# Page gathers issued once x has landed, compression weights loaded behind the first ada block, ada steps of the projection two tiles later

## What is computed

```
mod  = silu(c) @ w_ada + b_ada              # 2048 x 12288; shift1, scale1, gate1, shift2, scale2, gate2
h    = rmsnorm(x, norm1_g) * (1 + scale1) + shift1
p    = h @ w_in                             # queries, keys, values, gates, merge gates
past = cache_cmp_kv[page_table]             # 8 sequences x 16 pages x 128 rows: 2 MB each sequence
kvc  = gelu(blocks(past) @ cmp_w1 + pe @ cmp_w1) @ cmp_w2      # compression of the cached keys and values
m    = mixer(p, kvc, caches)                # compressed, selected, window and dilated attention
x    = x + gate1 * (m @ w_out)
x    = x + gate2 * swiglu(rmsnorm(x, norm2_g) * (1 + scale2) + shift2)
y    = rmsnorm(x, normf_g)
```

## Time and profile before

| | us |
|---|---|
| median of 3 runs | 1949.8 (1948.12 to 1950.07) |
| the profiled execution, its own time | 1946.32 |
| its span, first to last instruction | 1944.5 |
| PE busy | 1853.2 (95%) |
| DVE / ACT busy | 976.4 / 750.3 |
| mean granted PE clock | 0.980 |

### The profile page before, as it was taken

One profiled execution on the slowest core, in us unless ns is written; L12 is line 12 of the kernel. 1 busy time (PEld: TensorE's weight loads), 2 busy tenths in 40 slices (PEclk: granted clock), 3 DMA queues, 4 the chain that ended last, 5 costly groups with the idle time before them and its releaser, 6 DMA issues.

```text
span 1944.5 us, 35691 instructions
## 1 busy us (share of the span) xinstructions
PE 1853.2 (95%) x15365; PEld 1698.7 (87%) x15365; DVE 976.4 (50%) x1622; ACT 750.3 (39%) x1101; POOL 58.3 (3%) x108
## 2 busy tenths in 40 slices
PE   6988999999998879999999989999999999999997
PEld 4556899999954556999999989999999999999996
DVE  3437456654357533644456674444444444745454
ACT  2437333344344432533334343333333333633332
POOL 0000000000000000000000000000000000000000
PEclk9999999999999889999999999999999999999998
DMA  9991888887699857987788857777788777788881
GB/s 387 405 378 45 288 250 259 242 234 185 193 422 420 338 206 274 279 260 233 252 248 293 272 203 272 269 259 266 274 272 284 263 259 235 244 295 275 274 277 45
DMA packets 336549, 516.66 MB, mean 266 GB/s; under 512 B 8914, under 2 KB 310394, under 8 KB 319658
## 3 DMA queue, kind: packets, MB, share of 16 engines
q1 hardware_dynamic: 316306, 370.56, 57.4%
q0 software_dynamic: 5248, 125.73, 16.5%
q10 hardware_dynamic: 14896, 18.96, 3.6%
HBM read 506.32 MB, written 101.07 MB: 312 GB/s over the span
## 4 chain that ended last, share of the span: by engine, by line
PE 86%; DMA 6%; DVE 5%; ACT 2%; issue 1%; SPq 0%; ACTq 0%; DVEq 0%
PE bank L1217 19%; PE bank L1218 19%; PE bank L1219 19%; PE bank L893 5%; PE bank L894 5%; PE bank L895 5%; PE bank L784 4%; PE bank L821 3%; DMA piece<-in_w_ada 3%; DMA mem<-in_cache_win_kv 1%; PE bank L810 1%; DMA piece<-in_w_in 1%; PE bank L943 1%; DMA mem<-in_x_sample 1%; DMA x_kept<-mem 1%
## 5 line engine op out<-in xcount | busy, mean ns | idle before, releaser
L1217 PE MATMUL bank<-piece,piece 128*128 128x264 f32 x3040 | 863.9, 284 | 3.1 <-DVE piece L2210 2.0
L1218 PE MATMUL bank<-piece,piece 128*128 128x264 f32 x3040 | 864.6, 284 | 0.0
L1219 PE MATMUL bank<-piece,piece 128*128 128x264 f32 x3040 | 863.1, 284 | 0.0
L2215 DVE TENSOR_TENSOR piece<-piece,piece 128x2048 fp32r<-128x2048 f32 (+2 forms) x216 | 441.0, 2054 | 473.8 <-ACT piece L1648 473.8
L1648 ACT CAST piece<-piece 128x2048 fp32r<-128x2048 f32 (+2 forms) x216 | 369.1, 1716 | 549.6 <-PE bank L1219 499.0
L1217 PEld LDWEIGHTS bank<-piece,piece 128*128 128x128 f32 x3040 | 572.2, 188 | 4.2 <-DVE piece L2215 3.8
L1219 PEld LDWEIGHTS bank<-piece,piece 128*128 128x128 f32 x3040 | 572.4, 188 | 0.0
L1218 PEld LDWEIGHTS bank<-piece,piece 128*128 128x128 f32 x3040 | 571.7, 188 | 0.0
L893 PE MATMUL bank<-piece,piece 128*128 128x264 f32 (+1 forms) x816 | 235.0, 288 | 0.0
L894 PE MATMUL bank<-piece,piece 128*128 128x264 f32 (+1 forms) x816 | 232.2, 285 | 0.0
L895 PE MATMUL bank<-piece,piece 128*128 128x264 f32 (+1 forms) x816 | 231.6, 284 | 0.0
(11 more groups left out here) (345 smaller groups left out, 1309.6 us busy)
## 6 DMA issues: line engine op xcount, KB each, us to landing
piece<-in_w_ada SPq DMA_DIRECT2D x48, 2048.0 KB, 15.3
out_s_dil<-in_cache_dil_kv POOLq DMA_DIRECT2D x64, 1023.5 KB, 6.2
piece<-in_w_in SPq DMA_DIRECT2D x50, 1024.0 KB, 5.7
piece<-in_w_gate SPq DMA_DIRECT2D x22, 2048.0 KB, 9.8
piece<-in_w_up SPq DMA_DIRECT2D x22, 2048.0 KB, 8.1
piece<-in_w_down SPq DMA_DIRECT2D x32, 1408.0 KB, 6.7
piece<-in_w_in SPq DMA_DIRECT2D x16, 2048.0 KB, 8.8
piece<-in_w_out SPq DMA_DIRECT2D x8, 2048.0 KB, 8.5
```

What stands on the lines that cost most here:

```text
L1217: mm(out, w_high[:, k, :], half_tile(x_high[k]), start=(start and k == first_tile), stop=False)
L1218: mm(out, w_high[:, k, :], half_tile(x_low[k]), start=False, stop=False)
L1219: last = mm(out, w_low[:, k, :], half_tile(x_high[k]), start=False, stop=(stop and k == len(x_high) - 1))
L2215: v.tensor_tensor(half_chunk(a, k_tiles, f, CW), raw, half_chunk(buffer, k_tiles).bitcast(F32), ALU.subtract)\
```

## The change

Three moves, nothing in the arithmetic:

1. POOL's first gather waits for `x_loaded` (both loads of x) beside `runs`. The gathers of sequences 1 to 7 stand behind it in POOL's program with their waits as before.
2. `cmp_all` is issued by SP, between ada blocks 0 and 1, instead of by ACT.
3. Ada steps 16 to 23 stand behind tiles 5, 9, ..., 33 instead of 3, 7, ..., 31; the turn of their row moves from tile 32 to tile 34, and SP's loads of steps 17 to 24 come two chunks later. The load of step 16 stays where it is.

```diff
-    TILE_OF_STEP = {NA1 + i: 3 + i * 4 for i in range(NA2 - NA1)}
+    TILE_OF_STEP = {NA1 + i: 5 + i * 4 for i in range(NA2 - NA1)}
...
         for a in range(NA1):
+            if a == 1:
+                sp.dma_start(cmp_all, i_["cmp_all"]).then_inc(cmp_loaded, 16)
             if a == 3:
                 sp.dma_start(c_all[:, CONST_A:CONST_P], i_["const"][:, CONST_A:CONST_P]).then_inc(const_rest, 16)
...
             for u in range(B):
-                if u:
+                if u == 0:
+                    pool.wait_ge(x_loaded, 2 * 16)
+                else:
                     pool.wait_ge(*pe_.at(*{1: ("siluT",), 2: ("xT", KT - 1)}.get(u, ("used0", u - 2))))
...
-        act.dma_start(cmp_all, i_["cmp_all"]).then_inc(cmp_loaded, 16)
```

## The result

The changed kernel takes **1935.97 us** (median of 4 runs, 1934.18 to 1939.33) against 1949.93 (4 runs, 1948.12 to 1950.73): a ratio of 0.9932, interval 0.9915 to 0.9949, 14.0 us less. The direction was forecast; the time lies 3.5 us under the low end of the range. Over all sets of this study the kernel before ran 81 times, with a mean of 1949.8 and from 1942.7 to 1957.6, and the changed one 15 times, with a mean of 1938.2. By those means the change is worth **11.6 us**, give or take some 2.6 by their scatter, and 2.4 of the 14.0 are the luck of four runs.

What follows compares the result with a forecast made beforehand. Taken as bounds: DMA up to ada step 15, page copies by ACT and DVE to 199.55 us, PE's own work later. Move 3's 5.3 plus the start's 0.5 gave 5.8 us: 1949.8 to 1944.0, range 1939.5 to 1948.5.

Steps and rivals of the forecast that it cites:

- the lead: At the kernel's start: x lands, and PE reaches ada step 0, 4 us earlier through moves 1 and 2.
- the bounds of 3 to 6: Range for the earlier landing of x: 3 us if q1 misses some freed bandwidth, 6 if the landing delay shrinks.
- The Trainium skill's fit: For the load of x: about 2.0 us plus bytes at 436 GB/s, landing at 9.4 us, 5.8 us earlier.
- L764: Position matmuls near the start: claimed to begin at 29.4 us instead of 33.39.
- Move 3 was forecast at 5.3 us: Behind tile 3: removes PE's 3.75 us wait for ada block 16 and 1.56 us of slow-clock matmuls.
- the waits for `w_ada` ahead of step 16: Sign between 40 and 130 us: PE's waits for ada loads add up to some 9 us instead of 5.2.
- But the lead meets the DMA bound: Up to ada step 15: 51.2 MB must land first, so x's earlier landing mostly becomes waiting; step 15 at 129 to 130.
- 0.5 us was forecast for the start: Moves 1 and 2, up to ada step 15: gain from better use of the DMA engines, bounds 0 to 2.2 us.
- the lead passes through: Rival, up to ada step 15: PE's progress releases loads, so all 4 us arrive; 9.3 us saved, 1940.5 us; 17%.
- the signs named: In the changed profile, ada step 15 at 129 to 130 us would show the forecast right, at 126 wrong.
- the saving is the same there: Whole kernel: the median lies 3.5 us above the profiled execution, and the 5.8 us saving applies equally to it.
- The other rivals: Move 3 gives only 1 to 3.5 us (18%); or the DMA-bound stretch from 5 to 130 us gets slower (6%).

Runs made afterwards that it cites:

- m12_start_only: Kernel before with moves 1 and 2 alone (first gather after x, compression weights behind ada block 0): median 1946.11 us, ratio 0.9982.
- cut_before_short: Kernel before, cut off behind the projection, 30 of 32 position terms removed: median 535.65 us, against 538.76 for the cut kernel before.
- m3_tiles_only: Kernel before with move 3 alone (ada steps two tiles later): median 1943.16 us, ratio 0.9973.
- cut_after_late: Changed kernel, cut off behind the projection, 42 idle matmuls ahead of ada step 0: median 539.8 us, against 531.8 without them.
- the fillers: 24 idle matmuls in PE's waits at the end of the attention units: 1950.81 us (ratio 1.0001) in the kernel before, 1941.06 (0.9942) in the changed one.

## Why the prediction was wrong in size

**Right.** x at 11.2 was forecast, and it landed at 10.8, with the lead in this pair at 4.5; by several profiles of either start the lead at step 0 is 5.4, inside the bounds of 3 to 6. The Trainium skill's fit ("DMA: Bandwidth & Descriptors", Anatomy of one DMA) gave an estimate of 9.4 for the landing. That section gives the fit for transfers that GpSimd issues, and x is issued by SyncE. The trace says 10.8, so the measured landing stands and the estimate is 1.4 us short here. L764 was forecast at 29.4 and came at 28.93, ada step 0 at 37 and came at 36.33. Move 3 was forecast at 5.3 us and measured 5.1 over all profiles. Tile 4 follows tile 3 without a break, tile 6 didn't wait for its weights, and the step behind tile 5 ran at 2.4 GHz in 1.85 us. No gather and no position term became late. A smaller miss: the waits for `w_ada` ahead of step 16 were to grow from 5.2 to some 9 us, and grew to 6.7, since 3.0 us of the lead passed.

**Wrong, the first step: "But the lead meets the DMA bound".** 0.5 us was forecast for the start; the fixed points give 4.3, and more than 1 even at the low end of their scatter. The bytes were counted rightly. What was taken wrongly is that 50.86 MB at 407 GB/s is what the engines do in every execution, whenever PE comes. In the profiled execution they did: the share was 1.01 from 40 to 60 us. In five other profiles with the old start it was 0.86 to 0.91, since step 0 gave back its buffer too late. In 5 to 127 us the old start moved 48.7 to 50.3 MB, the changed kernel 50.8 twice. The rival "the lead passes through" had part of the mechanism, PE's progress releases the loads, and its sum of 9.3 us stands against the 9.4 of the profiles. The nearness is in part luck: the start gains by staying ahead of the hole, and not microsecond for microsecond, since arrivals from 36.3 to 38.4 us left step 15 at 127.0 to 129.9 in no order. It got 17% because one share in one window spoke against it. The window of 60 to 80 us at 377 GB/s, 46 below its neighbour in a stretch that was called full, might have raised a doubt, but it is no sign of a late arrival: `m12_start_only`, with step 0 at 36.5, moved 366 there. Of the signs named, step 15 at 126 for the rival and at 129 to 130 for the forecast, the profile after gave 127.00, nearer to the rival.

**Wrong, the second step: "the saving is the same there".** The profiled execution was 3.5 us under the median, and I took that as an offset without a cause. It had one, at least in part: x landed 1.3 us or more earlier than in the other five, and so step 0 escaped the hole. The execution at hand was the one in which the change has least to give. Profiles of before and after show 10.0 us between their spans (1.3 up to the end of tile 3, 5.1 in the projection, 3.6 behind it), the means of the runs 11.6.

**The miss summed.** 14.0 - 5.8 = 8.2 us: 3.8 for the start, -0.2 for move 3, 2.2 behind the projection (a remainder; its cause is open) and 2.4 for four runs of the changed kernel below its mean. Only the term of move 3 is known to a tenth; the others are good to 2 or 3 us. The other rivals did not come. Move 3 lost nothing elsewhere in the first 530 us, and the DMA rate did not fall with the gathers bunched; it rose.

## What to carry to other kernels

A byte sum that closes shows that the engines were busy in that execution, not that they are the limit: if the loads are released by the engine that waits for them, look for the instruction that frees the next buffer, and ask what happens when it comes one or two microseconds later. When the profiled execution is faster or slower than the median, find out where before saying that the saving is the same. Fixed points of a stage, read in several profiles of either kernel, sized the term of move 3, 5.1 us, to a tenth here, where the medians of twelve whole runs could not; the term of the start scattered by some 3 us even so. And a filler that is to take away a fall of the clock must be priced against the waits that it fills, or its own time hides what it gives back.

## What the runs showed of the hardware

- The load of x, 2.16 MB, landed at 15.2 us in one execution of the old start and at 16.6 to 17.9 in five others, with the same transfers issued beside it (and at 19.2 in `cut_before_short`). With `cmp_all` alone out of its way it landed at 11.8, with the gather alone at 14.9 (one profile each). With both out of its way it landed at 10.8 in the profiled execution of the changed kernel, and at 10.8 to 12.3 over the seven profiles with that start.
- A hole in the transfers was about as long as the load behind it was late: in `m3_tiles_only` load 3 was issued 1.8 us later than in before and the engines moved 371 instead of 416 GB/s from 40 to 60 us, which is 2.2 us of transfer; in `cut_after_late` it was issued 7.6 us later and they moved 257, which is 7.6 us.
- The granted clock fell in some executions and not in others behind the same waits of 2.4 and 1.23 us of PE. With the fall (a mean of 0.66 from 660 to 680 us) the same code took 19.0 us instead of 15.7; 24 idle matmuls in the waits took the fall away and made it 17.6.
- The 42 idle float32 matmuls of `cut_after_late` show as 84 in the trace and take 12.24 us, 0.146 each; the reckoning had counted 42. So one float32 matmul of the program with 128 columns costs 0.29 us there; in the fillers the 24 take 5.9 us, 0.25 each.
- Before lies within 15 us over 81 runs, and within 2.6 us over its first four: the narrow spread of a few runs was no measure of the kernel's.
